# Prompt attention of both branches and the sample's cached values in one part of eight interleaved steps

## The reference, cut to what matters

```
h = rmsnorm(x);  qA kA vA | qB kB vB | gate_a gate_b = h @ w_in
A (8 heads x 64), prompt:  z = q.k * scale + b_h, for keys before the query
      a = exp(log_sigmoid(z) - sum over later keys of softplus(z));   oA = a @ v
A, samples: the same over 4096 cached keys and values, gathered by page table
B (3 groups x 4 slots x 64), prompt: scores q.k * scale - slope * distance, masked to the group's
      window and dilation; softmax over the keys of all three groups together; yB = p @ v
B, samples: the same over 128 cached rows of each group
new caches of B: each group's cache moved up by one row, the sample's own row appended
x = x + (sigmoid(gate_a) * (oA @ w_br_a) + sigmoid(gate_b) * (yB @ w_br_b)) @ w_o
x = x + mixture of 32 experts (top 2);  y = rmsnorm(x)
```

## Time and profile before

| | us |
|---|---|
| median of three runs (lowest, highest) | 1586.48 (1580.89, 1590.81) |
| the profiled execution, its own time | 1582.86 |
| its span, first to last instruction | 1581.0 |
| attend_a | 414 to 636 |
| attend_b | 636 to 776 |
| decode_b | 776 to 824 |
| merge, first matmul to last | 827.5 to 945 |

### The profile page before, as it was taken

One profiled execution on the slowest core, in us unless ns is written; L12 is line 12 of the kernel. 1 busy time (PEld: TensorE's weight loads), 2 busy tenths in 40 slices (PEclk: granted clock), 3 DMA queues, 4 the chain that ended last, 5 costly groups with the idle time before them and its releaser, 6 DMA issues. The chain is left out here.

```text
span 1581.0 us, 14945 instructions
## 1 busy us (share of the span) xinstructions
PE 1269.2 (80%) x5502; PEld 750.8 (47%) x5502; DVE 585.3 (37%) x763; ACT 245.4 (16%) x401; POOL 291.6 (18%) x226
## 2 busy tenths in 40 slices
PE   4999999897567878789969995288878788887780
PEld 3878888786223434566537435233323233233230
DVE  2299999981622322333423114411111011111114
ACT  2111111001223232222100110011111011111112
POOL 1055555540033242100000000011111101001010
PEclk9999999999677898555569995589999999999895
DMA  6389989993677796755548008079999999999964
GB/s 205 131 290 343 331 301 340 352 355 123 257 287 312 313 360 278 266 199 207 216 177 317 2 0 338 0 295 407 411 407 408 408 406 408 403 406 405 408 271 178
DMA packets 99396, 455.41 MB, mean 288 GB/s; under 512 B 12752, under 2 KB 44800, under 8 KB 56560
## 3 DMA queue, kind: packets, MB, share of 16 engines
q1 hardware_dynamic: 73032, 300.09, 48.5%
q0 software_dynamic: 25776, 150.45, 25.0%
q10 hardware_dynamic: 544, 4.26, 0.7%
HBM read 442.10 MB, written 65.44 MB: 321 GB/s over the span
## 5 line engine op out<-in xcount | busy, mean ns | idle before, releaser
L419 PE MATMUL proj_ps<-hT,w_slots 128*128 128x260 f32 x1472 | 332.1, 386 | 10.2 <-ACT stage L442 8.0
L419 PEld LDWEIGHTS proj_ps<-hT,w_slots 128*128 128x128 f32 x1472 | 279.5, 192 | 60.6 <-issue 17.1
L1660 PE MATMUL ex_gp<-raw,ex_xT 128*64 128x512 f32 x1024 | 231.6, 600 | 19.8 <-DMA raw<-in_w_up_e 11.6
L1674 PE MATMUL ex_yp<-raw,ex_hmT 128*64 128x512 f32 x512 | 142.4, 707 | 67.1 <-DMA raw<-in_w_down_e 66.5
L205 POOL DMA_INDIRECT ring<-in_cache_k_a,run_sb x64 | 139.2, 2175 | 190.3 <-DVE scores L477 163.4
L470 DVE TENSOR_TENSOR ring<-ring,q_rep 128x2048 f32<-128x2048 f32 x64 | 145.9, 2281 | 40.6 <-ACT q_rep L461 40.6
L477 DVE TENSOR_REDUCE scores<-ring 128x32 f32<-128x2048 f32 x64 | 145.8, 2279 | 0.0
L1660 PEld LDWEIGHTS ex_gp<-raw,ex_xT 128*64 128x64 f32 x1024 | 70.6, 137 | 157.0 <-issue 124.3
L1674 PEld LDWEIGHTS ex_yp<-raw,ex_hmT 128*64 128x64 f32 x512 | 43.6, 160 | 163.3 <-issue 118.1
L1615 DVE TENSOR_TENSOR ex_hm<-ex_sg,ex_gp 64x512 f32<-64x512 f32 x32 | 21.7, 680 | 266.0 <-ACT ex_sg L1595 266.0
L205 POOL DMA_INDIRECT ring<-in_cache_v_a,run_sb x64 | 73.4, 1147 | 213.0 <-PE aa_vp L621 194.9
(11 more groups left out here) (241 smaller groups left out, 1101.0 us busy)
## 6 DMA issues: line engine op xcount, KB each, us to landing
raw<-in_w_gate_e SPq DMA_DIRECT2D x64, 1024.0 KB, 21.9
raw<-in_w_up_e SPq DMA_DIRECT2D x64, 1024.0 KB, 26.7
raw<-in_w_down_e SPq DMA_DIRECT2D x64, 1024.0 KB
o_kvs<-in_cache_kv_b SPq DMA_DIRECT2D x1, 32752.0 KB
w_slots<-in_w_in SPq DMA_DIRECT2D x23, 1024.0 KB, 9.0
o_kvs<-in_cache_kv_b SPq DMA_DIRECT2D x1, 8176.0 KB
kv<-in_cache_kv_b SPq DMA_DIRECT2D x24, 256.0 KB, 6.9
gate_rows<-stage SPq DMA_DIRECT2D x16, 260.0 KB, 8.9
```

What stands on the lines that cost most here:

```text
L419: last = pe.matmul(pp[:, j, half, 0:H], w[:, m % 2, c, j * P:(j + 1) * P], k.hT[:, c, half * H:(half + 1) * H], start=(c == 0), stop=(c == ...
L1660: last = pe.matmul(gp[at:at + SLOT, j], xT[:, c, :], raw[:, slot, c1 * FF:(c1 + 1) * FF], start=(c == 0), stop=(c == KC - 1))
L1674: last = pe.matmul(yp[h * SLOT:(h + 1) * SLOT, j], hmT[:, c, :], raw[:, slot, o:o + 512], start=(c == 0), stop=(c == FC - 1))
```

## The change

`attend_a` and `attend_b` become one part, `attend`. Its eight steps each hold head h of A, the values of sample h, and two units of B, with 13 or 14 blocks together (query blocks 3 and 0, or 2 and 1). Heads of B are read where `project` left them, also from partitions 64 to 127, and the copies on POOL and ACT are gone. PSUM's eight banks are: three for A's scores (one set in place of two), one for A's output, one for the values, one each for B's scores, transposes and products. So each of B's three pieces of scores waits for the bias of the one before, and A's next scores wait until DVE has subtracted the sums of this head. Line order on PE, DVE and ACT is written out by hand. The tables of B (`tables_b`) are loaded in `weigh_a`, ahead of the two copies there; SP issues the rest (`tables_d`), the `kv` loads and group 2's copy at the start of `decode_b`.

```diff
@@ -172,8 +172,12 @@
 
     def const(self, name, rows=P):
         a, b = self.at[name]
-        first = self.at["rel"][0]
-        return self.consts[0:rows, a:b] if b <= first else self.tables_b[0:rows, a - first:b - first]
+        first, second = self.at["rel"][0], self.at["row_bias"][0]
+        if b <= first:
+            return self.consts[0:rows, a:b]
+        if b <= second:
+            return self.tables_b[0:rows, a - first:b - first]
+        return self.tables_d[0:rows, a - second:b - second]
 
...
+        tables_in = k.sem("tables_in", ctx)
...
+                sp.dma_start(k.tables_b[:], k.io["consts"][:, k.at["rel"][0]:k.at["row_bias"][0]]).then_inc(tables_in, 16)
                 for g in range(NG - 1):
                     shift(k, sp, g)
+                sp.wait_ge(tables_in, 16)
...
+    FIRST = (lambda qb: max(qb - 1, 0), lambda qb: 0, lambda qb: 0)
+    WMAX = (2 + 2 * NB) * P
+    Q_TILE, K_TILE = 2 * WA // P, (2 * WA + WB) // P
+    UNITS = [(h // 2, qb) for h in range(HA) for qb in ((3, 0) if h % 2 == 0 else (2, 1))]
...
-        z = k.sb("aa_z", [P, 2, W], ctx=ctx)
-        soft = k.sb("aa_soft", [P, 2, W], ctx=ctx)
-        wt = k.sb("aa_w", [P, 2, PAGES, PAD], ctx=ctx)
-        om = k.sb("aa_own", [P, 2, WA], ctx=ctx)
...
-        zps = k.ps("aa_zp", [P, 2, 3 * SEQ], ctx)
-        vp = k.ps("aa_vp", [P, 2, WA], ctx)
...
+        z = k.sb("at_z", [P, 2, W], ctx=ctx)
+        soft = k.sb("at_soft", [P, W], ctx=ctx)
+        wt = k.sb("at_w", [P, 2, PAGES, PAD], ctx=ctx)
+        om = k.sb("at_own", [P, WA], ctx=ctx)
+        sc = k.sb("at_sc", [P, 2, WMAX], ctx=ctx)
...
+        zp = k.ps("at_zp", [P, 3 * SEQ], ctx)
+        op = k.ps("at_op", [P, SEQ], ctx)
+        vp = k.ps("at_vp", [P, WA], ctx)
+        sps = k.ps("at_sp", [P, 512], ctx)
+        tps = k.ps("at_tp", [P, 512], ctx)
+        mps = k.ps("at_mp", [P, 512], ctx)
...
+        def b_rows(slot, g, tile):
+            return k.qk[slot % 2 * HD:(slot % 2 + 1) * HD, tile + 2 * g + slot // 2, :]
...
                 def score(h):
-                    j = h % 2
-                    if h >= 2:
-                        pe.wait_ge(s["o_kept"], h - 1)
+                    if h >= 1:
+                        pe.wait_ge(s["less"], h)
...
-                score(0)
-                for h in range(HA):
-                    j = h % 2
-                    pe.wait_ge(s["w_laid"], h + 1)
-                    if h >= 2:
-                        pe.wait_ge(s["col_kept"], h - 1)
-                    values(h, range(0, 3))
-                    if h >= 1:
-                        columns(h - 1)
-                    if h + 1 < HA:
-                        score(h + 1)
+                def sums(h):
...
+                def score_b(n, g):
+                    slot, qb = UNITS[n]
+                    lo, _, w = pieces(qb)[g]
+                    if n or g:
+                        pe.wait_ge(s["biased"], n * NG + g)
+                    pe.matmul(sps[:, 0:w], b_rows(slot, g, Q_TILE)[:, qb * P:(qb + 1) * P],
+                              b_rows(slot, g, K_TILE)[:, lo * P:lo * P + w], start=True,
+                              stop=True).then_inc(s["b_scored"], 1)
...
+                def turn(n, lot):
+                    qb = UNITS[n][1]
+                    if lot >= len(lots(qb)):
+                        return
+                    if lot == 0:
+                        pe.wait_ge(s["b_exped"], n + 1)
+                    if lots_before[n] + lot:
+                        pe.wait_ge(s["laid"], lots_before[n] + lot)
+                    for c, blk in enumerate(lots(qb)[lot]):
+                        last = pe.transpose(tps[:, c * P:(c + 1) * P], sc[:, n % 2, blk * P:(blk + 1) * P],
+                                            k.const("ident"))
+                    last.then_inc(s["turned"], 1)
+
...
+                def mix(n):
+                    slot, qb = UNITS[n]
+                    pe.wait_ge(s["laid"], lots_before[n + 1])
+                    if n:
+                        pe.wait_ge(s["y_kept"], n)
+                    bl = blocks_of(qb)
+                    for c, (g, kb) in enumerate(bl):
+                        at = WA + g * WBO + slot * HD
+                        last = pe.matmul(mps[:, 0:HD], pt[:, n % 2, c * P:(c + 1) * P], k.v_rows[:, kb, at:at + HD],
+                                         start=(c == 0), stop=(c == len(bl) - 1))
+                    last.then_inc(s["mixed"], 1)
...
+                score(0)
+                for h in range(HA):
+                    a, b = 2 * h, 2 * h + 1
+                    sums(h)
+                    if h:
+                        columns(h - 1)
+                        mix(b - 2)
+                    score_b(a, 0)
+                    values(h, 0)
+                    if h + 1 < HA:
+                        score(h + 1)
+                    score_b(a, 1)
+                    values(h, 1)
+                    score_b(a, 2)
+                    out(h)
+                    values(h, 2)
+                    score_b(b, 0)
+                    values(h, 3)
+                    turn(a, 0)
+                    score_b(b, 1)
+                    values(h, 4)
+                    turn(a, 1)
+                    score_b(b, 2)
+                    values(h, 5)
+                    turn(a, 2)
+                    values(h, 6)
+                    mix(a)
+                    turn(b, 0)
+                    values(h, 7)
+                    turn(b, 1)
                 columns(HA - 1)
+                mix(len(UNITS) - 1)
+                for c in range(WBO // P):
+                    pe.wait_ge(s["y_kept"], len(UNITS))
+                    if c:
+                        pe.wait_ge(s["y_laid"], c)
+                    for qb in range(NB):
+                        last = pe.transpose(tps[:, qb * P:(qb + 1) * P], y[:, qb, c * P:(c + 1) * P], k.const("ident"))
+                    last.then_inc(s["y_turned"], 1)
...
+                def bias(n, g):
+                    slot, qb = UNITS[n]
+                    _, at, w = pieces(qb)[g]
+                    if n >= 2 and g == 0:
+                        dve.wait_ge(s["turned"], lots_before[n - 1])
+                    dve.wait_ge(s["b_scored"], n * NG + g + 1)
+                    i = g * SLOTS_B + slot
+                    dve.scalar_tensor_tensor(sc[:, n % 2, at:at + w], rel[:, g, SEQ - w:SEQ],
+                                             k.const("slope")[:, i:i + 1], sps[:, 0:w], ALU.mult, ALU.add)\
+                        .then_inc(s["biased"], 1)
...
+                dve.memset(wt[:], 0.0).then_inc(s["cleared"], 1)
+                first(0)
+                softplus(0)
+                for h in range(HA):
+                    a, b = 2 * h, 2 * h + 1
+                    if h:
+                        own(h - 1)
+                    less(h)
+                    bias(a, 0)
+                    if h + 1 < HA:
+                        first(h + 1)
+                    if h:
+                        keep(b - 2)
+                    bias(a, 1)
+                    bias(a, 2)
+                    most(a)
+                    bias(b, 0)
+                    if h + 1 < HA:
+                        softplus(h + 1)
+                    bias(b, 1)
+                    bias(b, 2)
+                    most(b)
+                    keep(a)
                 own(HA - 1)
+                keep(len(UNITS) - 1)
...
+                    exp_b(a)
+                    lay(a, 0)
+                    if h + 1 < HA:
+                        weights(h + 1)
+                    lay(a, 1)
+                    lay(a, 2)
+                    exp_b(b)
+                    lay(b, 0)
+                    lay(b, 1)
...
-            @block.gpsimd
-            def _(pool):
-
-                link = Chain(pool, moved)
-                with pool.Fori(0, TRIPS) as i:
-                    link.enter(i, 3 * NG)
-                    for j in range(2):
-
-                        pool.wait_ge(s["scored"], i * U + NB * (j + 1))
-                        rows = slice(j * HD, (j + 1) * HD)
-                        for g in range(NG):
-
...
+        kv_in = k.sem("kv_in", ctx)
         with nc.Block() as block:
+
+            @block.sync
+            def _(sp):
+                sp.dma_start(k.tables_d[:], k.io["consts"][:, k.at["row_bias"][0]:]).then_inc(kv_in, 16)
+                for b in range(DEC):
+                    for g, (_, d) in enumerate(GROUPS):
+                        sp.dma_start(k.kv[:, b, g, :], k.io[f"cache_kv_b{g}"][0, b].rearrange(
+                            "(n d) k h e -> n d (k h e)", d=d)[:, 0, :]).then_inc(kv_in, 16)
+                shift(k, sp, NG - 1)
 
             @block.tensor
...
-                dve.wait_ge(k.kv_in, 16 * DEC * NG)
+                dve.wait_ge(kv_in, 16 * DEC * NG + 16)
...
-STEPS = [prepare, project, weigh_a, attend_a, attend_b, decode_b, merge, route, experts, finish]
+STEPS = [prepare, project, weigh_a, attend, decode_b, merge, route, experts, finish]
...
```

(67 more changed lines are left out.)

279 lines of the change are left out of this document (59 added, 220 removed).

## The result

| | before | the change |
|---|---|---|
| median (lowest, highest) | 1588.64 (1580.89, 1591.18) | 1620.17 (1615.51, 1622.56) |
| profiled execution | 1582.86 | 1622.56 |
| the prompt's attention ends | 776 | 680 |
| decode_b ends | 824 | 744.6 |
| first matmul of merge | 827.5 | 868.7 |

The ratio of the changed kernel's times to those of before is 1.0203, with a 95% interval of 1.0157 to 1.025: slower by about 2%. The attention part is 96 us shorter than the two parts it replaces, and `merge` starts 41 us later. The profiled executions differ by 39.7 us.

What follows compares the result with a forecast made beforehand. PE was taken to bound both attention stages. Eight steps of 34.5 us end `attend` at 707; the copy, then uncovered, delays `merge` by 63.6 us: 1582.9 + 63.6 = 1646.5, given as 1646, range 1606 to 1680.

Steps and rivals of the forecast that it cites:

- The wait in `merge`: In `merge`, PE waits once for `mg_wb`, queued behind the copy on SP, for about 115 us.
- The rival by which the loads pass the copy: In `merge`, loads are served beside the copy, so it starts at 776; 1531 to 1580 us, chance 0.09.
- the landing: In `merge`, time from the copy's end to the first matmul: 2.5 us, with half of each load already through.
- The copy's own time: From `decode_b` into `merge`, group 2's copy needs 167.8 us from its issue, ending at 888.6.
- `decode_b`: After `attend`, DVE waits 17.7 us for `kv`, making the part 69 us, all under the copy.
- The waits in `attend`: PE waits each step 1.7 us for the bias before B's third piece and 1.2 before the first transposes.
- PE's work in a step: In `attend`, PE's matmul work at full clock sums to 29.05 us a step.
- Transposes of 13.5 blocks: In each `attend` step on PE, transposes priced like products of as many blocks, 3.3 us.
- I take 5.3: In each `attend` step on PE, sums over later keys priced at 5.3 us.
- B's scores: In each `attend` step on PE, 1664 or 1792 columns priced in the shape of A's scores, 3.3 us.
- a sign of being right: In `attend`, steps of 32 to 37 us from one run of sums to the next would show the forecast.
- without waits and at full clock: Favourable case for `attend`: it ends at 663, adding 20 us, for 1603 us in all.

Runs made afterwards that it cites:

- The order edit: Against the kernel with the 16-piece copy in `merge` (1528.48 us): B's second score piece and bias, and a values group, moved earlier in `attend`; 1526.61 us.

## Why the prediction was right, and where it was not

The forecast (1646, range 1606 to 1680, slower 0.87) has the right sign and mechanism; 1620.17 lies inside the range, 26 us below the number. The sign had a margin: `attend` ended at 680, and the two kernels would have been even with it at 643.4.

- **The wait in `merge`: right.** One wait of PE for `mg_wb`, 125.2 us (about 115 forecast), DMA at 0.51 all through it, the first matmul 4.4 us behind SP's release. With the copy left out it is 4.5 us. The rival by which the loads pass the copy did not come: half of the first three loads passed, and PE needs all of one. That half of each load would be through was right, though it did not shorten the landing.
- **The copy's own time: right within 4 us.** 171.8 us from its issue to SP's release, 167.8 priced. That it was hidden before is shown by the run of before without it.
- **`decode_b`: right in cause.** DVE waits 17.8 us for `kv` (17.7 priced). The part took 64.4 us where I said 69: the 51.2 that I started from ran to the first matmul of `merge`, and the part itself took 48.0 (776.3 to 824.3), to which 17.7 makes 65.7. All of it lies under the copy.
- **The waits in `attend`: right.** 13.4 and 6.0 us over seven steps are 1.9 and 0.86 a step, 2.8 together; priced 1.7 and 1.2, together 2.9.
- **PE's work in a step: the term that failed.** "Transposes of 13.5 blocks [...] I price a transpose the same: 3.3" put 0.244 us on a block from the products, and four blocks take 0.66, so 13.5 take 2.2. "I take 5.3" for the sums was a middle between 4.86 and 5.88, and they take 4.5 to 4.6: the lower bound itself was too high. Columns take 0.95, not 1.05. That is 2.0 us of 29.05. B's scores went the other way: the rows of the six pieces of 490 to 522 take 0.70, 1.02, 0.49, 0.48 and 0.48 us, and 1.57 for the one behind the wait, which at full clock would be another 1.02; that is 4.2 us, or some 3.8 without the overlap of each row with the next, and 3.3 was priced. So that 27.0 comes out is in part errors that cancel. In the six steps from 460.06 to 648.51 PE is busy for 172.0 us at a clock of 0.94, 28.7 a step, and 27.0/0.94 is 28.7; with 2.8 of waits it is 31.5, the step as measured from 427.76 to 648.51 in seven. Priced were 34.5, and 32 to 37 given as a sign of being right. The clock was not at fault: with the first step at 0.86 it is 0.92 over all seven, as forecast.
- **What that made of the sum.** `attend` ended at 680, not 707: 27 us. `kv` and the copy were issued 1.3 us sooner after it, the copy took 4.0 longer, the landing 1.9 longer: 891.1 less 27, less 1.3, plus 5.9 is 868.7. The start of `merge` moved by 41.2 us, not 63.6. `route` starts 38.8 later, and the rest ran as before.
- **The range** began at 1606, 3 us above the sum "without waits and at full clock", and the result lies 14 inside it: bounds that move eight times over made it wide, and an error of about 3 us a step, eight times over with one sign, placed the number high.

What stays open: whether the 1.2 us by which the output is longer behind the wait of 1.7 could be had back by closing that wait alone. The order edit took it away and a later one came in its place.

## What to carry to other kernels

A background transfer belongs to the last place where something covers it: before a part that covers one is shortened, look for what else it covers, and price the transfer's end against the next load wanted in the same queue. Give it whole stretches in which the DMA engines move next to nothing, in pieces no longer than each stretch, and look for the smallest load behind it, not the largest. Another queue is no way out where the copy has large packets and the other traffic small ones.

## What the runs showed of the hardware

- A DRAM-to-DRAM copy in 65 KB packets (33.5 MB, 520 packets with the eight small ones, the difference of the pages of the change with and without it) held 6 MB of `kv` loads in 2 KB rows for 178 and 174 us, from ACT's and from POOL's queue, though it filled half of the DMA engines (share 0.51); the same loads are issued in 12 us without it or ahead of it. From 700 to 850 the copy moved 455 packets and 29.80 MB, and `kv`'s queue 887 and 1.62 MB.
- In one queue, too, half of a load passes beside the copy (as I read it, the half on the engines that the copy leaves free): 640 of the 1280 rows of the first three loads of `mg_wb` moved by 774, and none from there to 862.
- SP's issue instruction itself lasts 24 and 94 us when earlier transfers of its queue are held: what looks like four loads in flight is an engine that can issue nothing more.
- In 16 pieces in place of 8 batches the copy went from a share of 0.51 and 200 to 210 GB/s to one of 0.93 to 0.99 and 313 to 332 GB/s, not 400.
